# Neighbourhood attention on TensorE: heads in pairs on halves of the array, the bias added by VectorE with the maximum, exps in SBUF

## The reference, cut to what matters

```python
def _na_context(h, w_in, q_g, k_g, w_out):
    q, k, v, g = _na_project(h, w_in, q_g, k_g)
    s = jnp.einsum('bhqd,bhkd->bhqk', q, k).astype(F32) * (C_DH ** -0.5)
    p = jax.nn.softmax(s, axis=-1).astype(v.dtype)
    o = jnp.einsum('bhqk,bhkd->bhqd', p, v).transpose(0, 2, 1, 3).reshape(bsz, t, D_MODEL)
    return (o * jax.nn.silu(g)) @ w_out, k, v
...
        s_loc = jnp.einsum('bhqd,bhrqwd->bhqrw', q_r, k_w).astype(F32) * scale + bias[None]
        s_ctx = jnp.einsum('bhqd,bhcd->bhqc', q_r, k_ctx).astype(F32) * scale
        s = jnp.concatenate([s_loc.reshape(bsz, C_HEADS, GRID_W, n_loc), s_ctx], axis=-1)
        p = jax.nn.softmax(s, axis=-1).astype(v.dtype)
        p_loc = p[..., :n_loc].reshape(bsz, C_HEADS, GRID_W, win_h, C_WIN_W)
        return (jnp.einsum('bhqrw,bhrqwd->bhqd', p_loc, v_w)
                + jnp.einsum('bhqc,bhcd->bhqd', p[..., n_loc:], v_ctx))
```

## Time and profile before

| | us |
|---|---|
| median of 3 runs (lowest, highest) | 1950.22 (1946.92, 1950.91) |
| span of the profiled execution | 1948.8 |
| TensorE busy with products | 1816.9, 93% |
| VectorE, ScalarE, GpSimd busy | 604.2, 495.2, 167.7 |

### The profile page before, as it was taken

How to read it: one execution, slowest core, us unless ns; L and a number is a source line. 1 busy time by engine, 2 the same in 40 slices (tenths; PEclk the granted TensorE clock), 3 DMA queues, 4 the chain that set the end, 5 groups by cost and what they waited for, 6 DMA issues and landing times.

```text
span 1948.8 us, 16614 instructions
## 1 busy us (share of the span) xinstructions
PE 1816.9 (93%) x6421; PEld 1050.9 (54%) x6421; DVE 604.2 (31%) x979; ACT 495.2 (25%) x960; POOL 167.7 (9%) x158
## 2 busy tenths in 40 slices
PE   6899999999989899988989998999799998898998
PEld 3355534755655554546455455545455536575655
DVE  0333005336340202375320552321433005445420
ACT  2201323323320114343111222231201223433300
POOL 1000001001000000052043000000100001100100
PEclk9999998999999998999999997999899999999999
DMA  6522222233242321242365221323222221212122
GB/s 189 203 86 86 88 74 76 76 112 116 83 146 95 113 86 43 76 150 98 130 126 156 86 86 44 98 98 110 73 86 87 99 74 44 83 48 87 44 88 75
DMA packets 105140, 185.98 MB, mean 95 GB/s; under 512 B 5136, under 2 KB 54704, under 8 KB 105072
## 3 DMA queue, kind: packets, MB, share of 16 engines
q1 hardware_dynamic: 95816, 158.40, 24.2%
q0 software_dynamic: 8640, 26.46, 4.6%
q10 hardware_dynamic: 616, 0.16, 0.1%
HBM read 164.47 MB, written 20.54 MB: 95 GB/s over the span
## 4 chain that ended last, share of the span: by engine, by line
PE 88%; DVE 5%; ACT 3%; issue 1%; DMA 1%; SPq 0%; DVEq 0%; ACTq 0%; POOLq 0%
PE acc L500 69%; PE mix L500 17%; PE acc L565 1%; DMA out_new_C<-cst 1%; DVE hT L1523 1%; ACT cp L1276 1%; DVE mix L1344 1%; DVE rd L1505 1%; DVE cstat L1666 1%; PE mix L915 0%; DMA ring<-in_a_w_out 0%; DMA cst<-in_c_k_g 0%; DVE dx L1590 0%; DVE hT L1348 0%; DVE fqk L1626 0%
## 5 line engine op out<-in xcount | busy, mean ns | idle before, releaser
L500 PE MATMUL acc<-hT,ring 128*128 128x385 f32 x1664 | 548.3, 491 | 15.8 <-DVE hT L1351 14.4
L500 PEld LDWEIGHTS acc<-hT,ring 128*128 128x128 f32 x1664 | 317.9, 192 | 244.6 <-issue 21.9
L500 PE MATMUL acc<-z,ring 128*128 128x385 f32 x512 | 169.5, 492 | 6.1 <-DMA ring<-in_a_w_out 4.2
L500 PE MATMUL acc<-ring,sc 128*2 128x384 f32 x512 | 170.2, 486 | 1.6 <-ACT mst L992 1.2
L500 PEld LDWEIGHTS acc<-z,ring 128*128 128x128 f32 x512 | 97.9, 192 | 77.7 <-issue 6.1
L500 PE MATMUL mix<-qs,ring 128*128 128x256 f32 x512 | 117.6, 392 | 9.6 <-DVE qs L1507 9.6
L500 PEld LDWEIGHTS mix<-qs,ring 128*128 128x128 f32 x512 | 100.1, 197 | 27.6 <-issue 13.2
L500 PEld LDWEIGHTS acc<-ring,sc 128*2 128x2 f32 x512 | 41.3, 85 | 119.1 <-issue 112.2
L1363 DVE SCALAR_TENSOR_TENSOR y<-acc,modv,y 128x128 f32 x64 | 23.4, 413 | 223.8 <-PE acc L500 223.8
L500 PE MATMUL acc<-ring,hT 128*128 128x512 f32 x192 | 85.5, 608 | 0.0
L500 PE MATMUL acc<-xc,bd 128*128 128x385 f32 x128 | 57.5, 574 | 14.2 <-DVE hT L1523 8.4
(11 more groups left out here) (297 smaller groups left out, 2212.6 us busy)
## 6 DMA issues: line engine op xcount, KB each, us to landing
ring<-in_w_mod SPq DMA_DIRECT2D x64, 768.0 KB, 6.2
ring<-in_a_w_in SPq DMA_DIRECT2D x32, 1024.0 KB, 6.9
ring<-in_state_mlstm_C SPq DMA_DIRECT2D x16, 1024.0 KB, 7.8
out_new_C<-cst POOLq DMA_DIRECT2D x32, 512.0 KB, 3.2
ring<-in_a_w_out SPq DMA_DIRECT2D x16, 1024.0 KB, 7.8
ring<-in_c_w_in SPq DMA_DIRECT2D x16, 1024.0 KB, 7.6
ring<-in_b_w_in SPq DMA_DIRECT2D x12, 1024.0 KB, 6.3
ring<-in_b_w_out SPq DMA_DIRECT2D x4, 1024.0 KB, 6.2
```

What stands on the lines that cost most here:

```text
L500: return nc.tensor.matmul(out, lhsT=lhsT, rhs=rhs, start=start, stop=stop)
```

## The change

What it does, engine by engine:

- TensorE: `scores(k)` now takes a pair of heads, with the five products of the even head (rows 0 to 63) and of the odd head (rows 64 to 127) in turn, each head into two banks of `mix` of its own. The product with the bias is gone. The scores of a pair wait for the maxima of the pair before (`mx_ready`), no longer for the exps. `values(k)` takes a pair too, the two heads' products in turn on the two halves of the columns. The order per pair is `scores(k + 1)`, `values(k - 1)`, `mod_part(k - 1)`, then both `turn`s.
- VectorE: `maxima(h)` reads the scores from PSUM, adds the bias, writes the sum to `cp` and takes the maximum in one operation (`tensor_tensor_reduce`); for the context part a multiplication by 1.0 with a maximum. In the order of the program each of the two new operations is followed by a small one that writes out its result.
- ScalarE: `exps(h)` reads and writes `cp` in SBUF. Per pair: both exps, the modulation's copies, both `turned`.
- Buffers: four of `cp` and `cstat`; `cp` and `cpt` lie in `cqr` and `ckrt`, so VectorE and ScalarE wait once for the norms (`qkn_ready`). The bias has 384 columns per head and half, the last 128 zero; GpSimd clears these, and VectorE, no longer TensorE, waits for `bias_ready`.

```diff
-            cb = sb("cb", 2 * CH * NLAT, stack=st)
...
-            cp = [sb(f"cp{s}", 896, stack=st) for s in range(2)]
-            cpt = [sb(f"cpt{s}", 896, stack=st) for s in range(2)]
-            cst_ = [sb(f"cstat{s}", 6, stack=st) for s in range(2)]
+            cst_ = [sb(f"cstat{s}", 6, stack=st) for s in range(4)]
...
+        cp = [(cqr, ckrt)[n // 3][:, seg_(n % 3 * 896, 896)] for n in range(4)]
+        cpt = [ckrt[:, seg_(n * 896, 896)] for n in (1, 2)]
...
-                def scores(h):
-
-                    k, r = h // 2, slice(64 * (h % 2), 64 * (h % 2) + 64)
-                    if h:
-                        pe.wait_ge(cx_ready, h)
-                    mm(mix[:, 0:P], cq3[r, k, 0:P], ck3[r, k, 0:P], True, True)
-                    for q in (1, 2):
-                        ps = mix[:, seg(q * 512, TC)]
-                        qt = cq3[r, k, seg(TOK[q], P)]
-                        mm(ps[:, 0:NLAT], qt, ck3[r, k, LAT:W], True, False)
-                        mm(ps[:, 0:NLAT], ident[:, :], cb4[:, q - 1, h, :], False, True)
-                        ins = mm(ps[:, NLAT:TC], qt, ckc[r, k * P:(k + 1) * P], True, True)
-                    ins.then_inc(cs_ready, 1)
+                def scores(k):
+
+                    if k:
+                        pe.wait_ge(mx_ready, 2 * k)
+                    for part in range(5):
+                        for e in range(2):
+                            r, c = slice(64 * e, 64 * e + 64), e * 1024
+                            q, first = (part + 1) // 2, part % 2
+                            if part == 0:
+                                ins = mm(mix[:, seg(c, P)], cq3[r, k, 0:P], ck3[r, k, 0:P], True, True)
+                            elif first:
+                                ins = mm(mix[:, seg(c + P + (q - 1) * TC, NLAT)], cq3[r, k, seg(TOK[q], P)],
+                                         ck3[r, k, LAT:W], True, True)
+                            else:
+                                ins = mm(mix[:, seg(c + q * TC, P)], cq3[r, k, seg(TOK[q], P)], ckc[r, k * P:(k + 1) * P],
+                                         True, True)
+                            if part == 4:
+                                ins.then_inc(cs_ready, 1)
...
-                        ins = nc.tensor.transpose(mix[:, seg(3 * 512 + b * P, P)], cp[h % 2][:, b * P:(b + 1) * P],
+                        ins = nc.tensor.transpose(mix[:, seg(4 * 512 + b * P, P)], cp[h % 4][:, b * P:(b + 1) * P],
...
-                def values(h):
-                    pe.wait_ge(cpt_ready, h + 1)
-                    k, r = h // 2, slice(64 * (h % 2), 64 * (h % 2) + 64)
-                    t = tile(f"attn{k}", l)
-                    ps = acc[t % 2]
-                    if h % 2 == 0:
-                        bank(t)
-                    hv = slice(h * CDH, (h + 1) * CDH)
-                    pt = cpt[h % 2]
-                    mm(ps[r, 0:P], cv3[:, 0, hv], pt[:, 0:P], True, True)
-                    for b, v in enumerate((cv3[:, 1, hv], cv3[:, 2, hv], cvc[:, hv])):
-                        both = pt[:, P:896].rearrange("p (q b t) -> p q b t", q=2, b=3)[:, :, b, :]
-                        ins = mm(ps[r, P:TC].rearrange("p (q t) -> p q t", q=2), v, both, b == 0, b == 2)
-                    if h % 2:
-                        ins.then_inc(acc_ready, 1)
+                def values(k):
+                    pe.wait_ge(cpt_ready, 2 * k + 2)
+                    ps = bank(tile(f"attn{k}", l))
+                    for b in range(4):
+                        for e in range(2):
+                            h, r, pt_ = 2 * k + e, slice(64 * e, 64 * e + 64), cpt[e]
+                            hv = slice(h * CDH, (h + 1) * CDH)
+                            if b == 0:
+                                ins = mm(ps[r, 0:P], cv3[:, 0, hv], pt_[:, 0:P], True, True)
+                            else:
+                                both = pt_[:, P:896].rearrange("p (q b t) -> p q b t", q=2, b=3)[:, :, b - 1, :]
+                                v = cvc[:, hv] if b == 3 else cv3[:, b, hv]
+                                ins = mm(ps[r, P:TC].rearrange("p (q t) -> p q t", q=2), v, both, b == 1, b == 3)
+                    ins.then_inc(acc_ready, 1)
...
-                pe.wait_ge(bias_ready, 1)
                 scores(0)
-                for h in range(CH):
-                    if h + 1 < CH:
-                        scores(h + 1)
-                    turn(h)
-                    if h:
-                        values(h - 1)
-                    if h and h % 2 == 0:
-                        mod_part(l + 1, h // 2 - 1)
-                values(CH - 1)
+                for k in range(KD):
+                    if k + 1 < KD:
+                        scores(k + 1)
+                    if k:
+                        values(k - 1)
+                        mod_part(l + 1, k - 1)
+                    for e in range(2):
+                        turn(2 * k + e)
+                values(KD - 1)
...
-                    if h >= 2:
-                        act.wait_ge(ct_ready, h - 1)
...
-                        ins = nc.scalar.activation(cp[s][:, seg(c, n)], mix[:, seg(q * 512, n)], ACT.Exp,
-                                                   bias=cst_[s][:, q:q + 1], accum_out=cst_[s][:, 3 + q:4 + q])
+                        ins = nc.scalar.activation(x[:, seg(c, n)], x[:, seg(c, n)], ACT.Exp,
+                                                   bias=st_[:, q:q + 1], accum_out=st_[:, 3 + q:4 + q])
...
-                for h in range(CH):
-                    exps(h)
-                    if h:
-                        turned(h - 1)
-                    if h >= 3 and h % 2:
-                        mod_part(l + 1, h // 2 - 1)
-                turned(CH - 1)
+                    nc.scalar.copy(cpt[h % 2], mix[:, seg(4 * 512, 896)]).then_inc(cpt_ready, 1)
+
+                act.wait_ge(qkn_ready, 2 * KD)
+                for k in range(KD):
+                    for e in range(2):
+                        exps(2 * k + e)
+                    if k:
+                        mod_part(l + 1, k - 1)
+                    for e in range(2):
+                        turned(2 * k + e)
...
-                    st_ = cst_[h % 2]
+                    st_, x, c = cst_[h % 4], cp[h % 4], h % 2 * 1024
+                    if h >= 4:
+                        dve.wait_ge(ct_ready, h - 3)
                     dve.wait_ge(cs_ready, h + 1)
-                    for q, n in enumerate((P, TC, TC)):
-                        ins = nc.vector.tensor_reduce(st_[:, q:q + 1], mix[:, seg(q * 512, n)], AX, ALU.max)
+                    nc.vector.tensor_scalar(x[:, 0:P], mix[:, seg(c, P)], 1.0, None, ALU.mult, ALU.max,
+                                            accum_out=st_[:, 0:1])
+                    for q in range(2):
+                        ins = nc.vector.tensor_tensor_reduce(x[:, seg(P + q * TC, TC)], mix[:, seg(c + P + q * TC, TC)],
+                                                             cb4[:, q, h, :], 1.0, -BIG, ALU.add, ALU.max,
+                                                             st_[:, 1 + q:2 + q])
                     link(ins)
                     nc.vector.tensor_scalar(st_[:, 0:3], st_[:, 0:3], -1.0, None, ALU.mult).then_inc(mx_ready, 1)
...
-                maxima(0)
-                for h in range(CH):
-                    normalise(h)
-                    if h + 1 < CH:
-                        maxima(h + 1)
-                    if h and h % 2 == 0:
-                        gated(h // 2 - 1)
+                dve.wait_ge(bias_ready, 1)
+                dve.wait_ge(qkn_ready, 2 * KD)
+                for k in range(KD):
+                    for e in range(2):
+                        maxima(2 * k + e)
+                    for e in range(2):
+                        normalise(2 * k + e)
+                    if k:
+                        gated(k - 1)
...
+                nc.gpsimd.memset(cb4[:, :, :, NLAT:TC], 0.0)
...
-                both = cb.rearrange("p (n c) -> p n c", c=GW)
-                nc.gpsimd.tensor_tensor(both, both, cwin.unsqueeze(1).to_broadcast([P, 2 * CH * ROWS, GW]), ALU.add
-                                        ).then_inc(bias_ready, 1)
+                for q in range(2):
+                    both = cb4[:, q, :, 0:NLAT].rearrange("p h (r c) -> p h r c", c=GW)
+                    ins = nc.gpsimd.tensor_tensor(both, both, cwin.unsqueeze(1).unsqueeze(1).to_broadcast(
+                        [P, CH, ROWS, GW]), ALU.add)
+                ins.then_inc(bias_ready, 1)
```

More of the change, by code:

```diff
@@ L152, in trunk, with seg_ @@
         V_N0 = 3 * P
+        def seg_(col0, n):
+            return slice(col0, col0 + n)
         def v3(t, n, w=W):
@@ L249, in trunk @@
             ckrt = sb("ckrt", KD * W, stack=st)
-            cb = sb("cb", 2 * CH * NLAT, stack=st)
+            cb = sb("cb", 2 * CH * TC, stack=st)
             cwin = sb("cwin", GW, stack=st)
@@ L1281, in turned @@
                     act.wait_ge(ct_ready, h + 1)
```

(14 more changed lines are left out.)

2 lines of the change are left out of this document (1 added, 1 removed).

## The result

| | us |
|---|---|
| median after, 4 runs (lowest, highest) | 1897.12 (1895.0, 1904.74) |
| median before, 4 runs beside them | 1949.3 (1946.92, 1950.91) |
| ratio, 95% interval | 0.9745, 0.9723 to 0.9767 |
| the profiled execution after: time, span | 1904.74, 1903.0 |

The change makes the kernel faster by 52 us; 1906 was predicted, 1896 to 1926 given as the range. The profiled execution is the longest of the four. The same kernel, run once more with the experiments, had a median of 1902.51, ratio 0.9767 (0.9748 to 0.9786). So the gain is 46 to 52 us, and a difference of 5 us between two kernels is read from the stage in their traces, not from two medians of different chips alone.

What follows compares the result with a forecast made beforehand. TensorE was taken as the bound, with 88% of the chain. The attention falls from 149.5 to 105 us (−44.6), the span from 1948.8 to 1904.2; with 1.4 over the span, 1906 us, range 1896 to 1926.

Steps and rivals of the forecast that it cites:

- Scores of a pair: TensorE's score products for two heads: 1.70 us if the row halves run side by side, 3.2 if not.
- Values: TensorE's value products for two heads, alternating on column halves: 1.65 us a pair in place of 3.4.
- Modulation: TensorE's modulation work in each pair stays: 5.5 us, made of 5.2 and 0.27 for its columns.
- Turns: Two heads' transposes sharing one PSUM place, the second waiting for ScalarE's copy: 2.9 us a pair, 1.08 of it waiting.
- A pair: TensorE's period per pair of heads in the attention: 1.70 + 1.65 + 5.5 + 2.9 = 11.8 us.
- The start: First pairs, maxima uncovered: TensorE idle 3.4 us, clock low from 5.4 to 27 us, turns of the first pairs done at 32.1.
- The end: Last pair, without scores to cover ScalarE's second copy: 11.1 us, then the last copy and values 2.7.
- (b): Rival: TensorE's clock falls in each pair because transposes don't keep it, 6.0 us more a pair, 1942; chance 0.05.
- (a): Rival: row halves take turns in the scores, 3.2 us a pair, stage 117 us, 1918; chance 0.13.
- (e): Rival: pairing does nothing, halves run one after the other, 1930, or 1955 if each alternation cost 0.2; chance 0.05.
- (c): Rival: half-array work counts as little, clock low through the whole stage, 173 us, 1973, slower; chance 0.04.
- (d): Rival: VectorE becomes the bound, a head's maxima 5.9 us, a pair 15.9, 1935; chance 0.05.

Runs made afterwards that it cites:

- half-by-half runs: The change with all products of the even head before the odd head's: scores 1914.6 us, values 1906.0, both 1917.6.
- the change again: The changed kernel itself, unaltered, run once more beside the experiments: median 1902.5 us, ratio 0.9767.
- exps ahead: Against the paired kernel with bias on TensorE and exps reading PSUM: the next pair's exps precede this pair's copies in ScalarE's list; 1928.2 us.

## Why the prediction was right, step by step

The number was 9 us above the first median and 3.5 above the second; the mechanism is the predicted one, and the sizes of a pair held. That the profiled execution (1904.7) lies 1.3 us from 1906 is luck: up to the last modulation part the stage took 99.5 us (1183.45 to 1282.93) where 105 were forecast, and the rest of the program was some 4 us longer than in the profile before.

- *Scores of a pair* 1.70: measured 1.73. *Values* 1.65: 1.66. *Modulation* 5.5: 5.53. *Turns* 2.9: 2.96, 1.09 of it waiting. *A pair* 11.8: 11.88. Row halves overlap as column halves did; that was the step without a row of its own, and the half-by-half runs show it: 0.98 for the scores, 0.70 for the values. The Trainium skill ("TensorEngine Tiling (Array Packing)", Key Properties) says that different tiles can load weights and multiply at the same time; the trace agrees, at 1.73 where the same columns would need 3.0 one after another.
- *VectorE* 1.7 us for a head's maxima: measured 1.36, since the read-outs of the sums, put at 0.1 each, add 0.02 or less, and the two sums start 0.48 apart where 0.55 was taken. It is hidden in the pairs either way.
- *ScalarE*: exps from SBUF 0.60 for 384 columns, where 0.57 was measured from PSUM; hidden.
- ***The start was the term that was mis-sized.*** I let the clock fall at 5.4 us and return at 27, as it had before, and got 32.1 us to the fourth scores; it was 25.3 and 23.6. The fall came, but lasted 3.4 us at a time. The run with the first three scores half by half gives the forecast's picture: low for 20.4 us, and 32.1. That the two 32.1 agree so closely is luck, since there the third scores came 1.0 us later and took 5.16 for 3.4, and the values, modulation and turns 12.4 for 15.2. So the step that missed is one assumption: that the low stretch would be as long as that of the kernel before, whose scores came one half at a time, with the bias on 128 rows between. With it went 7 to 8.5 us. The same sum with the clock never low was the 97 us of the prediction's lower end (by its own terms 105 − 8.6, so nearer 96.4); the change again took 96.9.
- Within the start, the third scores were put at 13.5 us, behind turns at half pace. They come at 12.0, and what sets them is VectorE's list behind the first exps and the table load, which I didn't see.
- *The end*: 13.8 us were forecast from the end of the five full periods to the end of the last values; it took 13.9 in the change again (1265.53 to 1279.4), and 14.8 in the first profile (1268.10 to 1282.93), where the clock fell once more there. With the start (−6.9) and five pairs (+0.4) this accounts for the 99.5: 105 − 6.9 + 0.4 + 1.0.
- *Nothing lost elsewhere*: the span fell by 45.8 where the stage fell by 49.3; in the change again 51.3 and 52.5. These few us in other stages move from one execution to the next; what moves them is not shown, and the same holds for those by which medians and stages differ above (2 to 6 us).
- *Two readings behind rival (b), without effect on the sum.* The prediction has 16-row products run for the 10 us at 0.50. They ran from 732.55 to 741.30, and the clock fell at 736.3; from 741.30 on, for the second half of that stretch, products on 128 rows ran. And 0.21 us a transpose is the pace of the low clock (seven take 1.48 us at 0.50 and 0.93 at 1.00 in the first profile); what speaks against (b) there is that the products right behind twenty transposes already have full pace.

Rivals: (a) and (e) fell with 1.73 and 1.66, (b) and (c) with the clock at 1.00 for 81.8 us, (d) with 0.55 us for the new operation.

The share of the two halves of the change can be told apart now, against the change again (1902.5, stage 103.7): undoing the order of the halves costs 15 us by the median and 21 by the stage, putting the bias back on TensorE 26 and 28 (exps ahead), and, with the lists left as they are, 56 and 61. No run within the pairs' order undoes both at once, so whether the two prices add up to the whole gain is not shown. With the exps' source in SBUF, their place in ScalarE's list no longer holds up the scores.

## What to carry to other kernels

- Two products on different halves of the array overlap when they alternate in the queue; issued half by half, 0.98 of some 1.3 us was lost for the scores and 0.70 of some 1.35 for the values, and behind the wait at the start it also kept the clock low for 20.4 us in place of 3.4.
- When a stage gets dense, read its start and its end by themselves: here 5 us of independent work moved into the first wait, and a copy hidden behind half a modulation, gave another 12 to 15 us by the stage, 13 to 18 by the median.
- Before a bound is put down to a resource, look at what stands ahead in the waiting engine's list: 30 us of "bias on TensorE" were the place of the exps on ScalarE.

## What was unexpected of the hardware

- The length of the clock's low stretch at the start: 3.4 us once or twice with the two row halves in turn (6.8 and then 3.4 where the maxima were doubled or the bias was on TensorE with the exps ahead), 20.4 us with the same products half by half (three kernels, and the kernel before). Why the order of the halves matters for it was not measured.
- Issued half by half, two heads' scores still take 2.71 us, not 3.0: the seam between the heads overlaps.
- VectorE's sum with a maximum over 384 columns, one operand in PSUM, takes 0.55 us, and two of them start 0.48 apart with their read-out between.
